# Latent up products and head work mixed into the short units of the second attention

## What is computed

```
q  = (rms_norm(c_q)  @ w_uq ).reshape(B, S, 8, 64 + 32)
kv = (rms_norm(c_kv) @ w_ukv).reshape(B, S, 8, 64 + 64)
q_nope, k_nope = rms_norm(q[..., :64]), rms_norm(kv[..., :64])
q_rope = rope(rms_norm(q[..., 64:]));  v = kv[..., 64:]
q_full = concat(q_nope, q_rope);  k_full = concat(k_nope, k_rope)
p = softmax(mask(q_full @ k_full.T / sqrt(96)));  mla = p @ v
```

## Time and profile before

| | us |
|---|---|
| median of 3 runs (lowest, highest) | 1568.82 (1567.87, 1568.86) |
| the profiled execution, its own time | 1569.52 |
| its span, first to last instruction | 1567.7 |
| TensorE (PE) busy | 1450.9 (93%) |
| VectorE (DVE) busy | 1028.8 (66%) |
| ScalarE (ACT) busy | 890.8 (57%) |
| latent stage, first product to first row scored | 451.30 to 524.89 |
| unit 0 of the second attention starts | 549.33 |
| unit 3, the last short one, starts | 595.65 |

### The profile page before, as it was taken

How to read it: one execution, slowest core, us unless ns; L and a number is a source line. 1 busy time by engine, 2 the same in 40 slices (tenths; PEclk the granted TensorE clock), 3 DMA queues, 4 the chain that set the end, 5 groups by cost and what they waited for, 6 DMA issues and landing times.

```text
span 1567.7 us, 21242 instructions
## 1 busy us (share of the span) xinstructions
PE 1450.9 (93%) x7417; PEld 1109.4 (71%) x7417; DVE 1028.8 (66%) x1896; ACT 890.8 (57%) x1598; POOL 182.1 (12%) x243
## 2 busy tenths in 40 slices
PE   6999999987889699999999999996999999999996
PEld 5888988343446344447877888885878888888885
DVE  4512126698759767666873433347788999988887
ACT  6321566676757545664333333342677888788776
POOL 0000000456620000000000000000111112111111
PEclk9999999998999789999999999996999999999998
DMA  6200225410020000012130010033898666666794
GB/s 215 58 27 14 83 83 215 154 38 1 1 108 1 1 0 28 31 51 81 41 134 0 30 52 28 27 135 121 288 369 279 213 203 205 222 220 216 224 376 143
DMA packets 87299, 184.81 MB, mean 118 GB/s; under 512 B 14272, under 2 KB 24512, under 8 KB 86464
## 3 DMA queue, kind: packets, MB, share of 16 engines
q1 hardware_dynamic: 77952, 161.90, 29.0%
q0 software_dynamic: 7200, 22.03, 5.5%
q10 hardware_dynamic: 2080, 0.01, 0.1%
HBM read 216.42 MB, written 26.21 MB: 155 GB/s over the span
## 4 chain that ended last, share of the span: by engine, by line
PE 71%; DVE 9%; DMA 8%; ACT 5%; issue 4%; POOL 1%; DVEq 0%; ACTq 0%; SPq 0%; POOLq 0%
PE psum L1794 28%; PE psum L2025 17%; DMA up_stage<-in_w_up 8%; PE psum L1778 8%; PE psum L1921 6%; PE psum L1942 4%; PE psum L1771 3%; PE psum L1908 3%; DVE up_rest L1460 3%; POOL arena L712 1%; DVE gate_rest L1460 1%; DVE mx L1423 1%; PE psum L2074 1%; PE psum L2170 1%; ACT gate_high L1073 1%
## 5 line engine op out<-in xcount | busy, mean ns | idle before, releaser
L1921 PE MATMUL psum<-arena 64*128 64x512 f32 (+7 forms) x384 | 124.3, 546 | 20.6 <-ACT arena L1044 12.0
L1460 DVE TENSOR_TENSOR down_rest<-down_stage,down_high 128x1024 fp32r<-128x1024 f32 x96 | 115.0, 1218 | 28.2 <-ACT down_high L1073 28.2
L1460 DVE TENSOR_TENSOR up_rest<-up_stage,up_high 128x1024 fp32r<-128x1024 f32 x100 | 117.0, 1219 | 15.9 <-ACT up_high L1073 15.6
L1921 PEld LDWEIGHTS psum<-arena 64*128 64x128 f32 (+1 forms) x384 | 50.4, 197 | 102.3 <-issue 47.2
L1778 PE MATMUL psum<-arena 128*128 128x512 f32 (+2 forms) x352 | 119.2, 491 | 0.8 <-DVE arena L1366 0.8
L1942 PEld LDWEIGHTS psum<-ident,arena 128*128 128x128 f32 x576 | 70.3, 152 | 67.0 <-ACT arena L777 33.1
L1460 DVE TENSOR_TENSOR gate_rest<-gate_stage,gate_high 128x1024 fp32r<-128x1024 f32 x100 | 115.6, 1216 | 1.2 <-ACT gate_high L1073 1.2
L1794 PE MATMUL psum<-up_high,rows_high 128*128 128x256 f32 x384 | 110.5, 288 | 6.0 <-DVE up_rest L1460 5.7
L777 ACT ACTIVATE arena<-psum 128x512 f32<-128x512 f32 (+1 forms) x192 | 85.8, 501 | 49.4 <-PE psum L1942 49.3
L1073 ACT ACTIVATE up_high<-up_stage 128x1024 fp32r<-128x1024 f32 x100 | 100.3, 1059 | 23.6 <-DMA up_stage<-in_w_up 23.6
L1942 PE MATMUL psum<-ident,arena 128*128 128x128 f32 x576 | 93.3, 302 | 20.7 <-DVE arena L1382 14.3
(11 more groups left out here) (363 smaller groups left out, 3635.4 us busy)
## 6 DMA issues: line engine op xcount, KB each, us to landing
gate_stage<-in_w_gate SPq DMA_DIRECT2D x25, 2048.0 KB
up_stage<-in_w_up SPq DMA_DIRECT2D x25, 2048.0 KB
down_stage<-in_w_down SPq DMA_DIRECT2D x24, 2048.0 KB
arena<-in_x SPq DMA_DIRECT2D x16, 512.0 KB, 3.6
arena<-in_w_mkv SPq DMA_DIRECT2D x8, 1024.0 KB, 6.2
arena<-in_w_in SPq DMA_DIRECT2D x4, 1024.0 KB, 10.4
arena<-in_w_mo SPq DMA_DIRECT2D x4, 1024.0 KB, 6.5
mv_times_w_mo_spill<-arena SPq DMA_DIRECT2D x8, 512.0 KB, 2.8
```

Of the source, the lines that this page charges most:

```text
L1460: ins = dve.tensor_tensor(split[part][1][:, k, :], stage[part][:, k, :], split[part][0][:, k, :].bitcast(F32), ALU.subtract)
L1921: mm = pe.matmul(pair(1 + a)[:, at:end], lhs, rhs(at, end), start=True, stop=True)
```

## The change

The latent loop does tiles 0 to 5 and turns the heads of tiles 0 to 3. The products of tiles 6 and 7 stand between the row pairs of unit 0 (TensorE: `last_tiles`; ScalarE: behind rows 1, 3, 5, 7), with the turned heads of tile 4. VectorE's work for a tile is cut in four (`head_squares`, `head_roots`, `heads_normed`, `heads_rotated`); tiles 5, 6 and 7 are done in pieces behind rows 1, 3, 5 and 7 of units 0, 1 and 2. The heads of tile 5 are turned in unit 0, of tile 6 in unit 1, of tile 7 in unit 2: kf in step 1 and qf in step 2, at the end of the step, on TensorE behind the scores, on ScalarE behind the exponentials. The list of rounds has them there too, so the number k of a unit's own round is counted apart (`round_number`). Short rows are scored into one bank each (2 + a), since banks 4 to 7 are still used by the products; the first long row waits for the last short exponential. The short rows' probabilities lie in other buffers (unit 0's where w_o is loaded, so that this load waits for unit 0 to be turned).

```diff
+UP_FIRST = 6
...
+def late_heads(u, j):
+    return (("kf", "qf")[j - 1], UP_FIRST - 1 + u) if u <= T - UP_FIRST and j in (1, 2) else None
+def round_number(kind, u, j, a):
+    return sum(2 * blocks(kind, v) for v in range(u)) + 2 * j + a
...
-    for i in range(T):
+    for i in range(UP_FIRST - 1):
         add("kf", i, "act")
         add("qf", i, "act")
     for u in range(N_UNITS):
         for j in range(blocks("mla", u)):
             for a in range(2):
                 rounds.append((("mla", u, j, a), "act"))
+            if late_heads(u, j):
+                add(*late_heads(u, j), "act")
...
+        p_short = {}
+        at = 44288
+        for r in range(GRP):
+            for b in range(2):
+                for a in range(2):
+                    n = P * (r + 1)
+                    if r == 0 and b == 0:
+                        p_short[r, a, b] = cut(40960 + n * a, n)
+                    elif not (b and last_row("mla", r)):
+                        p_short[r, a, b] = cut(at, n)
+                        at += n
+        p_first = {(r, a): cut(P * (r * (r + 1) + (r + 1) * a), P * (r + 1)) for r in range(GRP) for a in range(2)}
+        def probs_of(u, r, a):
+            if u == 0:
+                return p_first[r, a]
+            return p_row(u, r, a) if u >= PAIRS else p_short[r, a, 0 if last_row("mla", r) else u % 2]
...
+        def scores_of(kind, u, a):
+            return bank(2 + a) if kind == "mla" and u < PAIRS else pair(1 + a)
...
-            sp.wait_ge(s_o, N_UNITS)
+            sp.wait_ge(s_t, LAST["mla", 0] + 1)
...
+                    if kind == "mla" and n in (1, 5):
+                        latent_kv_taken(UP_FIRST + n // 4)
+                    if kind == "mla" and n in (3, 7):
+                        if n == 3:
+                            up_turned("kf", GRP)
+                        latent_q_taken(UP_FIRST + n // 4)
+                        if n == 3:
+                            up_turned("qf", GRP)
...
                         for k in plan.get(j, ()) if more else ():
                             one(ROWS * (u + 1) + k)
+                        if kind == "mla" and late_heads(u, j):
+                            up_turned(*late_heads(u, j))
...
+            for i in range(UP_FIRST):
+                latent_kv_taken(i)
                 if i >= 2:
                     up_turned("kf", i - 2)
-                if i < T:
-                    act.wait_ge(s_p3, 2 * i + 2)
-                    if i >= 3:
-                        act.wait_ge(s_t, ROUND[("qf", i - 3, 1)] + 1)
-                    for half in range(2):
-                        hs = slice(4 * half, 4 * half + 4)
-                        src = bank(4 + half)[:, 0:4 * QK].rearrange("p (a b) -> p a b", a=4)
-                        do(act.activation(sq_q[:, i % 2, hs, :], src, ACT.Square, scale=rq))
-                        do(act.activation(qf[:, hs, :], src, ACT.Copy, scale=rq), s_q3 if half else None)
+                latent_q_taken(i)
                 if i >= 2:
                     up_turned("qf", i - 2)
...
+                late = UP_FIRST - 1 + n // ROWS
+                if late < T:
+                    if n % ROWS == 1:
+                        head_squares(late)
+                    if n % ROWS == 3:
+                        head_roots()
+                    if n % ROWS == 5:
+                        heads_normed(late)
+                    if n % ROWS == 7:
+                        heads_rotated(late)
...
+                    if kind == "mla" and j == 0 and u < 2:
+                        pe.wait_ge(s_q3, 2 * T - 1)
...
+                    if kind == "mla" and rows_[0][0] == ROWS * PAIRS:
+                        pe.wait_ge(s_free, ROWS * PAIRS)
+                        pe.wait_ge(s_q3, 2 * T)
+                        pe.wait_ge(s_te["act"], EMPTIED[ROUND[("qf", T - 1, 1)]][1])
                     for at in range(0, L, 512):
                         for n, r, a in rows_:
                             end = min(L, at + 512)
                             lhs, rhs = scores(p, a, GRP * g + r)
-                            mm = pe.matmul(pair(1 + a)[:, at:end], lhs, rhs(at, end), start=True, stop=True)
+                            mm = pe.matmul(scores_of(kind, u, a)[:, at:end], lhs, rhs(at, end), start=True, stop=True)
...
                         if j in SCORE_STEPS[kind, nj]:
                             scores_at(u + 1, SCORE_STEPS[kind, nj][j])
+                        if kind == "mla" and late_heads(u, j):
+                            which, i = late_heads(u, j)
+                            pe.wait_ge(s_qkf, i + 1)
+                            turn_up(which, i)
...
+            for i in range(UP_FIRST):
+                latent_kv(i)
                 if i >= 2:
                     pe.wait_ge(s_qkf, i - 1)
                     turn_up("kf", i - 2)
-                if i < T:
-                    if i >= 1:
-                        pe.wait_ge(s_q3, 2 * i)
-                    for half in range(2):
-                        product(bank(4 + half)[:, 0:4 * QK],
-                                [(cT[:, k, at], w_q[:, k, 4 * QK * half:4 * QK * (half + 1)]) for k in range(3)],
-                                s_p3 if half else None)
+                latent_q(i)
                 if i >= 2:
                     turn_up("qf", i - 2)
-            def last_tile(i):
-                if i == 0:
-                    pe.wait_ge(s_qkf, T)
-                    turn_up("kf", T - 1)
-                    turn_up("qf", T - 1)
-                if i == 3:
-                    pe.wait_ge(s_te["act"], EMPTIED[ROUND[("qf", T - 1, 1)]][1])
-            pe.wait_ge(s_q3, 2 * T)
+            def last_tiles(step):
+                i = UP_FIRST + step // 2
+                if step % 2 == 0:
+                    latent_kv(i)
+                    return
+                if step == 1:
+                    pe.wait_ge(s_qkf, GRP + 1)
+                    turn_up("kf", GRP)
+                latent_q(i)
+                if step == 1:
+                    turn_up("qf", GRP)
```

More of the change, by code:

```diff
@@ L954, in spread @@
                 i = ROUND[kind, u, j, a]
-                k = i - ROUND[kind, 0, 0, 0]
+                k = round_number(kind, u, j, a)
                 lo = P * max(0, j - GRP * UNITS[kind][u][1])
@@ L1002, in up_turned, with latent_kv_taken @@
                                       scale=gk96[0:QK, 0:1] if kind == "kf" else 1.0), s_te["act"])
-            for i in range(T + 2):
-                if i < T:
[L1006 to L1010, removed]
-                    if i >= 3:
-                        act.wait_ge(s_t, ROUND[("kf", i - 3, 1)] + 1)
-                    for half in range(2):
-                        hs = slice(4 * half, 4 * half + 4)
[L1015 to L1019, removed]
+            def latent_kv_taken(i):
+                rkv, kf = crst[:, T + i:T + i + 1], kfs[i % 3]
+                act.wait_ge(s_p3, 2 * i + 1)
+                if i >= 2:
+                    act.wait_ge(s_red, i - 1)
+                if i >= 3:
+                    act.wait_ge(s_t, ROUND[("kf", i - 3, 1)] + 1)
+                for half in range(2):
+                    hs = slice(4 * half, 4 * half + 4)
+                    kv = bank(6 + half).rearrange("p (a b) -> p a b", a=4)
+                    do(act.activation(sq_k[:, i % 2, hs, :], kv[:, :, 0:NOPE], ACT.Square, scale=rkv))
+                    do(act.activation(kf[:, hs, 0:NOPE], kv[:, :, 0:NOPE], ACT.Copy, scale=rkv))
+                    do(act.activation(v_mla[:, i, 4 * half * HD:(4 * half + 4) * HD].rearrange("p (a b) -> p a b", a=4),
+                                      kv[:, :, NOPE:NOPE + HD], ACT.Copy, scale=rkv), s_q3 if half else None)
@@ new lines, in latent_q_taken @@
+            def latent_q_taken(i):
+                rq, qf = crst[:, i:i + 1], qfs[i % 3]
+                act.wait_ge(s_p3, 2 * i + 2)
+                if i >= 3:
+                    act.wait_ge(s_t, ROUND[("qf", i - 3, 1)] + 1)
+                for half in range(2):
+                    hs = slice(4 * half, 4 * half + 4)
+                    src = bank(4 + half)[:, 0:4 * QK].rearrange("p (a b) -> p a b", a=4)
+                    do(act.activation(sq_q[:, i % 2, hs, :], src, ACT.Square, scale=rq))
+                    do(act.activation(qf[:, hs, :], src, ACT.Copy, scale=rq), s_q3 if half else None)
@@ L1043, in exps @@
                     act.wait_ge(s_pn, n - 3)
-                do(act.activation(p_row(u, r, a)[:, 0:L], pair(1 + a)[:, 0:L], ACT.Exp, scale=QK ** -0.5,
+                do(act.activation(probs_of(u, r, a)[:, 0:L], scores_of("mla", u, a)[:, 0:L], ACT.Exp, scale=QK ** -0.5,
                                   bias=nb[:, n % 4:n % 4 + 1], accum_out=rs[:, n % 4:n % 4 + 1]), s_e)
@@ L1389, in _, with head_squares @@
                 out_rows("sb", u, s_pv, s_o, 0)
-            for t in range(T):
+            def head_squares(t):
                 dve.wait_ge(s_q3, 2 * t + 2)
-                qf, kf = qfs[t % 3], kfs[t % 3]
```

(26 more changed lines are left out.)

26 lines of the change are left out of this document (15 added, 11 removed).

## The result

| | before | changed |
|---|---|---|
| median (lowest, highest), us | 1568.82 (1567.02, 1569.06), 5 runs | 1577.63 (1573.50, 1580.30), 5 runs |
| the profiled execution | 1569.52 | 1573.50 |

The ratio is 1.0055 [1.0036, 1.0074]: 0.55% slower, 8.8 us by the medians, where 1573.9 with a range of 1562 to 1580 had been forecast. A second series of the changed kernel gave 1576.26 in 12 runs, ratio 1.0044 [1.0026, 1.0063]. The profiled execution is the fastest of its five.

What follows compares the result with a forecast made beforehand. It took TensorE to bound the latent stage and VectorE's maximum and scale the short units. -22.6 ahead of unit 0, +18.1 in the units and +9.6 for the clock gave +5.1, 1573.9 us; range 1562 to 1580.

Steps and rivals of the forecast that it cites:

- Ahead of unit 0, -22.6: Latent stage's end and unit 0's rows: interleaved products let unit 0 start at 526.75 instead of 549.33, -22.6 us.
- Units at the full clock, +18.1: Units 0 to 2 at full clock: 64.4 us in all for 46.32 before, +18.1 us.
- the bank waits: Steps 2 and 3 of short units: TensorE idles 1.5 to 2.9 us each until ScalarE's copy empties the transposition banks.
- the long row: End of unit 2: the first long row waits for the last short exponential, 1.5 us more than before.
- rival 2: Short units: bank waits hidden, VectorE sets the units, 57 us for 64.4; -11.9, 1556.9 us; chance 0.08.
- Clock, +9.6: Units 0 to 2: new gaps put TensorE at half clock more often, +9.6 us, within bounds of 0 and 15.6.
- (a): Unit start to row 2's maximum: 5.0, 5.7 and 4.2 us in units 0 to 2; half clock adds 2.9.
- (b): Row 2's maximum to row 4's: 5.8 us where it was 2.50; half clock adds 3.5 over three units.
- (c): Row 4's maximum to row 6's: 5.9 us where it was 2.91; half clock adds 2.3 over three units.
- the tail: Row 6's maximum to next unit's start: 4.1 us as before, 4.7 in unit 2; half clock adds 0.9.
- rival 1: The clock holds in the new units: -4.5 us, 1564.3 us, faster; chance 0.18.
- the 0.75 named: Sign in the short units: mean clock under 0.75 for the forecast, over 0.85 if the clock holds.

Runs made afterwards that it cites:

- run 9: Changed kernel with ScalarE's copies first, banks 2 and 4 from unit 2 on, and two idle products before unit 0's first rows: 1556.28 us, ratio 0.9905.
- run 4: Changed kernel with two idle 512-wide products behind each turning of heads in units 0 to 2: 1569.34 us, ratio 0.9993.
- run 1: Changed kernel with ScalarE's copies of turned heads put ahead of the exponentials of the same step: 1567.25 us, ratio 0.9992.
- run 2: Changed kernel without VectorE's roots and norm of the heads of tiles 5, 6 and 7: 1573.94 us, ratio 1.0034.
- run 5: Changed kernel with ScalarE's copies ahead of the exponentials and rows in banks 2 and 4 from unit 2 on: 1557.88 us, ratio 0.9923.

## Why the prediction was right

The sign and the two sides of the sum were right, the size was short by 3.7 us by the medians (+5.1 forecast, +8.8 and then +5.7 measured) and by 2.8 within the stretch (7.9 in the profile; 1.9 with the 7.0 of the second profile). An error of this size is below the 4.7 us by which two profiles of the changed kernel differ behind the stretch, so that the median came so near its number is in part luck.

- *Ahead of unit 0, -22.6.* Measured -21.7. The order came out as worked; the product of tile 6 took 5.19 us for 3.4 to 3.6, since the clock fell behind the gap of 2.17 us. That was named and left in the range; 1.7 us of it came, and run 9 takes it away.
- *Units at the full clock, +18.1.* This term holds the bank waits, VectorE's added work and the long row together; against the prediction's own rival 2 the waits are only 7.4 of it (64.4 against 57). The waits are there: TensorE stands for 11.1 us, released by L1044, twice in each unit. The step from row 2 to row 4 measured 5.94 in unit 1 (558.11 to 564.05) and 5.87 in unit 2, both at the upper clock, for my 5.8. Unit 0 of run 4, all at the full clock, is 21.38 for my 20.8. Moving the copies takes 11.8 us from the units (run 1), taking VectorE's work away 0.2 (run 2). No run has all three units at the full clock, so the term as a whole was not measured by itself.
- *Clock, +9.6.* Of the 75.87 us, 11.5 are over the 64.4 of the full clock. By pieces of the prediction, over the three units, (a) came 2.8 over its full-clock value (2.9 taken), (b) 2.0 (3.5), (c) 3.6 (2.3) and the tail 3.0 (0.9). So this term is the one mis-sized, by 1.9; it was 1.5 too high in (b) and 3.4 too low in (c) and the tail, and the errors partly cancelled. Unit 2 has most of it: the start was at half (6.2 us to row 2, for 4.2 at full and 6.4 at half), row 2 to row 4 wasn't (5.87), row 4 to row 6 was (7.59, for 5.9 and 7.3), the tail was (8.97 behind row 6, for 6.2 and 9.1). Run 4 takes 6.6 us back by filling the gaps. The Trainium skill (TensorE: Matmul & The Clock Gate, Part 1) ties the fall to an idle stretch, and the prediction read it so that none of these gaps is one. The trace does not agree with that reading: the clock fell five times between 503.49 and 604.61, four times behind gaps of 2.05 to 2.17 us, once, at 550 to 551, behind gaps of 1.18 and 0.70; and the fall of the earlier trace rows lies in a gap of 0.70 us (562.82 to 563.52).
- *What is left.* Of the 29.6 us, filling alone gives back 6.6, copies first alone 11.8 (with the clock that its shorter gaps bring back), and copies first with the banks 15.7 (60.17 in run 5). 13.9 us over the units of before remain. They hold the turning in the line of the scores, VectorE's head work (in units 0 and 1 of run 5 VectorE waits for scores for 0 and 0.3 us) and what is left of the half clock; the runs do not separate these.
- *Rivals.* The clock did not hold (rival 1; 0.83, 0.71, 0.68, in mean 0.74, under the 0.75 named). VectorE did not set the units (rival 2; run 2, and its 20.4 us of waiting).
- *What was wrong.* The prediction says that all behind the first long unit is to be unchanged, and that it is wrong in kind if the time differs there. It did differ, by 5.0 us. But that sign was badly chosen: one and the same kernel differs by 4.7 us there between two profiles (967.1 and 971.8), so a single execution says nothing at that level. Of the other signs, unit 2 with 28.66 us is outside the 21 to 25 given. Also wrong was that with the copies first unit 2 would fall to 17 us, in run 1: the turning itself is in the scores' line, and the long row's wait (3.8 us by runs 1 and 5) came on top.

## What to carry to other kernels

Filling one engine's idle stretch with work from later is worth its length only if the work that moved is not put into somebody's queue between a producer and a consumer: ask of each instruction of every engine what is behind it, and for shared ping-pong buffers, which copy frees them and what that copy stands behind. Here the stretch ahead of the units became 21.7 us shorter and the kernel still 8.8 us slower; another order on ScalarE and another choice of bank, with the same work in the same steps, made it 12.0 us faster than the kernel before in its series (run 5). And a chain of short waits can cost TensorE's clock besides (6.6 us here): look at the granted clock of the stretch beside the waits.

When edits differ by a few us, take two profiles of one kernel first. Here they differed by 4.7 us in code that no edit touches.

## What the runs showed of the hardware

Adding 12 idle 512-wide products to the three units made the kernel 8.3 us faster by the medians; the granted clock in unit 0 went from 0.83 to 1.00 (run 4). The clock fell in unit 0 right behind 2.05 us without a matmul. In the kernel before it fell in a gap of only 0.70 us, behind 10 us in which TensorE was busy for 8.84; in units 1 and 2 of the changed kernel gaps of 1.91 us left it at 1.00 (558 to 564 and 582 to 588). So a longer gap can pass without a fall and a shorter one have it: the length of the gap before it does not tell. Two profiles of the same kernel took 967.1 and 971.8 us for the same code, at mean clocks of 0.98 and 0.97.
